# Two transformer blocks on one core: norms, a feed-forward entry and the last group in another order, six PSUM banks for the up-projection, and TensorE work in its pauses

## What is computed

```python
def rmsnorm(x, gain):
    var = jnp.mean(x * x, axis=-1, keepdims=True)
    return x * lax.rsqrt(var + 1e-6) * gain

# layer 1, its end
x = x + rmsnorm(merged @ w_out, norm_mix_post)
h = rmsnorm(x, norm_ffn_pre)
up = h @ w_up                       # 1024 -> 2 * 2816
conv = conv_b + sum(conv_w[i] * shifted(up, 2 - i) for i in range(3))
gate, val = jnp.split(conv, 2, axis=-1)
f = (gelu(gate) * val) @ w_down     # layers 2 and 3: silu in place of gelu
x = x + rmsnorm(f, norm_ffn_post)
# layer 2 begins with proj = rmsnorm(x, fox_norm) @ w_fox_in
# layer 3: v = (latent @ w_uv), 16 heads of 128
# the end
out = rmsnorm(x, final_norm)
```

## Time and profile before

| | us |
|---|---|
| median of 3 runs | 2248.14 (2243.22 to 2248.35) |
| the profiled execution | 2245.98 |
| its span, first to last instruction | 2244.2 |
| TensorE busy | 2174.7, 97% of the span |
| VectorE, ScalarE, GpSimd busy | 1176.3, 903.1, 934.9 |
| share of the chain that ended last | TensorE 89%, VectorE 6%, ScalarE 3%, DMA 1% |

### The profile page before, as it was taken

One profiled execution on the slowest core, in us unless ns is written; L12 is line 12 of the kernel. 1 busy time (PEld: TensorE's weight loads), 2 busy tenths in 40 slices (PEclk: granted clock), 3 DMA queues, 4 the chain that ended last, 5 costly groups with the idle time before them and its releaser, 6 DMA issues.

```text
span 2244.2 us, 26145 instructions
## 1 busy us (share of the span) xinstructions
PE 2174.7 (97%) x10426; PEld 1784.7 (80%) x10426; DVE 1176.3 (52%) x1713; ACT 903.1 (40%) x1381; POOL 934.9 (42%) x726
## 2 busy tenths in 40 slices
PE   8999999988999998999999999999999999999997
PEld 6877788866888877777788888887888888888886
DVE  5775333567666106676466662167666424666511
ACT  5214432353433224576444332254445334433322
POOL 5333435534444443322444444453222244454442
PEclk9999999999999998999999999999999999999998
DMA  5221223322333332211333233322111233333332
GB/s 176 69 71 58 79 71 99 103 75 75 100 98 92 98 102 66 75 57 39 95 102 94 94 101 95 96 94 67 50 54 51 62 95 96 101 94 96 97 94 80
DMA packets 57913, 191.48 MB, mean 85 GB/s; under 512 B 6448, under 2 KB 8640, under 8 KB 57792
## 3 DMA queue, kind: packets, MB, share of 16 engines
q1 hardware_dynamic: 57792, 189.81, 26.9%
HBM read 187.69 MB, written 2.10 MB: 85 GB/s over the span
## 4 chain that ended last, share of the span: by engine, by line
PE 89%; DVE 6%; ACT 3%; DMA 1%; issue 1%; ACTq 0%; POOL 0%; DVEq 0%; SPq 0%
PE ps L572 25%; PE ps L574 25%; PE ps L573 25%; PE ps L1039 2%; PE ps L625 1%; PE ps L937 1%; PE ps L626 1%; PE ps L627 1%; DMA RAW<-weights 1%; PE ps L928 1%; DVE TURNED L1552 1%; PE ps L992 1%; DVE CV L1555 1%; PE ps L678 1%; PE ps L961 1%
## 5 line engine op out<-in xcount | busy, mean ns | idle before, releaser
L564 POOL TENSOR_TENSOR WLO<-RAW,WHI 128x512 fp32r<-128x512 f32 (+1 forms) x722 | 934.6, 1320 | 1278.5 <-ACT WHI L1127 1278.0
L1127 ACT ACTIVATE WHI<-RAW 128x1024 fp32r<-128x1024 f32 (+2 forms) x374 | 373.1, 1001 | 666.9 <-DMA RAW<-weights 491.1
L572 PE MATMUL ps<-HH,WHI 128*128 128x512 f32 x1200 | 476.2, 397 | 26.2 <-POOL WLO L564 9.1
L574 PE MATMUL ps<-HH,WLO 128*128 128x512 f32 x1200 | 469.4, 391 | 0.0
L573 PE MATMUL ps<-HL,WHI 128*128 128x512 f32 x1200 | 469.3, 391 | 0.0
L572 PEld LDWEIGHTS ps<-HH,WHI 128*128 128x128 f32 x1200 | 226.8, 189 | 79.0 <-issue 12.5
L1555 DVE SCALAR_TENSOR_TENSOR CV<-U,PAR,CV 128x512 f32<-128x512 f32 x264 | 267.5, 1033 | 8.5 <-ACT CV L1342 3.9
L573 PEld LDWEIGHTS ps<-HL,WHI 128*128 128x128 f32 x1200 | 226.9, 189 | 48.8 <-issue 2.4
L574 PEld LDWEIGHTS ps<-HH,WLO 128*128 128x128 f32 x1200 | 226.5, 189 | 47.8
L1552 DVE TENSOR_TENSOR U<-ps,RSTD 128x512 f32<-128x512 f32 x132 | 90.5, 688 | 247.6 <-PE ps L574 224.2
L573 PE MATMUL ps<-ACTL,WHI 128*128 128x512 f32 (+1 forms) x550 | 209.3, 381 | 0.0
(11 more groups left out here) (314 smaller groups left out, 3305.5 us busy)
## 6 DMA issues: line engine op xcount, KB each, us to landing
RAW<-weights SPq DMA_DIRECT2D x300, 512.0 KB, 3.5
RAW<-weights SPq DMA_DIRECT2D x48, 384.0 KB, 3.0
RAW<-weights SPq DMA_DIRECT2D x26, 256.0 KB, 2.6
X<-xT SPq DMA_DIRECT2D x4, 512.0 KB, 6.5
outT<-X SPq DMA_DIRECT2D x8, 256.0 KB, 2.2
RESET<-resets SPq DMA_DIRECT2D x1, 512.0 KB, 10.8
CS<-rope SPq DMA_DIRECT2D x1, 512.0 KB, 3.7
M8F<-masks SPq DMA_DIRECT2D x1, 448.0 KB, 10.0
```

Of the source, the lines that this page charges most:

```text
L564: pool.tensor_tensor(WLO[:, slot, w], RAW[:, slot, w], WHI[:, slot, w].bitcast(F32), ALU.subtract).then_inc(w_lo, 1)
L572: pe.matmul(out, wh, hh, start=first, stop=False)
L574: return pe.matmul(out, wl, hh, start=False, stop=last)
L1127: act.activation(WHI[:, slot, 0:cols], RAW[:, slot, 0:cols], ACT.Copy).then_inc(w_hi, 1)
```

## The change

- **Banks**: gate.q and val.q of all three feed-forward networks get banks 2 (q mod 3) and 2 (q mod 3) + 1. The other groups keep their alternation of 0 and 1.
- **TensorE work in pauses**: four fp32 matmuls of a zeroed tile ahead of the first product, and 24 bf16 matmuls of a mask (`keep_clock`) behind `stats_in_two` in both block norms. Their results are not read.
- **Block norms**: VectorE clears SUMSQ ahead of the wait for RSTD and not behind the first two `scaled`; ScalarE loads the Ln table ahead of the last square (`early_table`); the cast of one chunk stands behind the second high tile and not ahead of the first.
- **Entry of feed-forward 0**: `stats` comes 12 matmuls earlier; ScalarE's casts of gate.2 to val.3 stand in other places of q = 0.
- **Latent attention**: the values of pair 0 are computed ahead of the first pair, with a weight chunk of their own (375 chunks, not 374).
- **The last group**: the sums for the first half stand in the second half, behind its block 6; VectorE scales six tiles of the first half ahead of adding the second.

```diff
+    tokens(["mv0.0", "mv0.1"], "mv0", 0, 2 * LORA_K)
     for p in range(MLA_H // 2):
...
@@ bank_table
             b = 2 + int(group[-1])
+        elif group[:4] in ("gate", "val0", "val1", "val2"):
+            b = int(group.split(".")[1]) % 3 * 2 + (group[0] == "v")
         else:
             b, turn = turn, 1 - turn
@@ tensor
+            def keep_clock(n):
+                for _ in range(n):
+                    pe.matmul(ps[:, 6, :], M16[:, 0:P], M16[:, 0:T], start=True, stop=True)
...
+            pe.wait_ge(zeroed, 1)
+            for _ in range(4):
+                pe.matmul(ps[:, 7, :], QT[:, 0:P], QT[:, 0:T], start=True, stop=True)
...
             stats_in_two("mixpost", 8)
+            keep_clock(24)
...
                     for at in range(4):
-                        for name in UP0_HEAD:
+                        for n, name in enumerate(UP0_HEAD):
+                            if at == 3 and n == 2:
+                                stats(site, 8)
                             part(name, at, *h, by_tile(site))
-                    stats(site, 8)
...
             stats_in_two("ffnpost", 8)
+            keep_clock(24)
...
             group("qn.1", *CQ_)
+            mla_values(0)
             for p in range(MLA_H // 2 - 1):
...
+                        if n and k == 6:
+                            pe.wait_ge(sumsq, SQ_AT["final"] + KD + 1)
+                            for m, part_ in enumerate(TOKEN_HALVES):
+                                pe.matmul(ps[:, HALF_SUM[m], part_], ones, SUMSQ[:, part_], start=True, stop=False)
+                            last_sum(0)
                 mm.then_inc(half_done, 1)
...
+            last_sum(1)
@@ scalar
+            def early_table(func):
+                warmed[0] += 1
+                act.activation(WARM[:, :], con("one"), func).then_inc(warm, 1)
+                act.wait_ge(warm, warmed[0])
...
                 else:
+                    early_table(ACT.Ln)
                     act.wait_ge(lin_done, DONE[f"{stage}.{j}"])
                     square(j, j % 2, ps[:, BANK[f"{stage}.{j}"], :], site)
...
-            casts(chunk_of("gate0.0"))
-            each_tile(lambda j, k: (act.wait_ge(x_done, j + 1), h_tile(j, k, "ffnpre0", "ffnpre0")))
+            for j in range(KD):
+                act.wait_ge(x_done, j + 1)
+                h_tile(j, j % 2, "ffnpre0", "ffnpre0")
+                if j == 1:
+                    casts(chunk_of("gate0.0"))
...
-                        casts(chunk_of(name) + 3 if f or q > 1 else chunk_of("gate0.2") + 3 + q)
+                        if f or q:
+                            casts(chunk_of(name) + 3 if f or q > 1 else chunk_of("gate0.2") + 3 + q)
+                        elif m == 0:
+                            casts(chunk_of("val0.2"))
...
+                    if f == 0 and q == 0:
+                        casts(chunk_of("gate0.2") + 3)
@@ vector
+            dve.memset(QT[:, 0:T], 0.0).then_inc(zeroed, 1)
...
             def post_norm(site, nxt, done):
+                clear_sum(nxt)
+                dve.sem_inc(sumsq, 1)
                 scale_known(site)
-                dve.sem_inc(sumsq, 1)
...
                 scaled(1)
-                clear_sum(nxt)
...
             drain_q(1)
+            drain_values(0, 0)
+            drain_values(0, 1)
             query_lo(1).then_inc(head_ready, 1)
...
+            last_add(0)
+            last_scaled(0, range(6))
+            last_add(1)
+            last_scaled(0, range(6, KD))
+            last_scaled(1, range(KD))
```

More of the change, by code:

```diff
@@ L161, in linear_plan @@
             whole(f"qn.{a}", QLORA_K)
-        values = [(f"mv{p}.{half}", f"mv{p}", 0, 2 * LORA_K, 0) for half in range(2)]
+        values = [(f"mv{p}.{half}", f"mv{p}", 0, 2 * LORA_K, 0) for half in range(2)] if p else []
         if p < MLA_H // 2 - 1:
@@ L1353, in _ @@
             root("ffnpost", D, RSTD)
-            casts(chunk_of("fv0.0"))
-            each_tile(lambda j, k: (act.wait_ge(x_done, j + (KD + 1)), h_tile(j, k, "fox", "fox")))
+            for j in range(KD):
+                act.wait_ge(x_done, j + (KD + 1))
+                h_tile(j, j % 2, "fox", "fox")
+                if j == 1:
+                    casts(chunk_of("fv0.0"))
             casts(chunk_of("foxf"))
@@ L1380, in _ @@
             act.activation(FZ[:, 1, :], FZ[:, 1, :], ACT.Ln, bias=con("one")).then_inc(f_act, 1)
-            act.activation(WARM[:, :], con("one"), ACT.Exp).then_inc(warm, 1)
-            act.wait_ge(warm, 2)
+            early_table(ACT.Exp)
             casts(chunk_of("fv1.3") + 3)
@@ L1519, in _ @@
             query_hi(1)
-            casts(chunk_of("qn.1") + 3)
+            casts(chunk_of("mv0.0") + 3)
             for p in range(MLA_H // 2 - 1):
```

28 lines of the change are left out of this document (16 added, 12 removed).

## The result

The changed kernel takes 2231.74 us (median of 4 runs, 2229.13 to 2233.17); the kernel before takes 2245.91 beside it (4 runs). The ratio is 0.9931 with a 95% interval of 0.9919 to 0.9943: faster by 14.2 us. That is inside the forecast range of 2219 to 2236, and 5.7 us above the forecast of 2226. The profiled execution is the fastest of the four, 2229.13 with a span of 2227.3; against the 2245.98 and 2244.2 of before that is 16.9 us in the pair of traces, where the prediction's terms add up to 20.5.

The account below looks back on a forecast made before the run. TensorE, busy 97% of the span, bounds the kernel; only its pauses and slow stretches, some 70 us of 2244, can be saved. Terms sum to -20.5 from 2245.98, giving 2225.5, rounded up to 2226; range 2219 to 2236.

Parts of the forecast that it names:

- start: Program start: fp32 matmuls ahead bring full clock, so seven slow first products run faster, -1.4 us.
- norm behind wout, first product: Block norm behind wout: VectorE's savings of 1.75 against Ln's +0.5 bring the first product 1.25 us earlier.
- the same norm, tiles behind it: Low tiles behind wout's norm: half clock saved, -1.9, against a wait for the fourth tile, +1.2; -0.7 us.
- feed-forward 0, wait and clock: Gate.4 no longer waits for gate.3's bank, -8.4 - 0.2, and the half clock behind goes, -2.1 us.
- late weights of val.4: Feed-forward 0: val.4's cast stands behind round 2 on ScalarE, so TensorE waits +0.6 us, between 0 and 3.
- three drains just begun: Starts of gate1.0, down0.0 and down1.0: each waits 0.95 us for a bank just left, +2.85 us in all.
- norm behind down0: Second block norm: Ln +1.3, VectorE -1.75, clock -2.45, wait for the fourth tile +1.2; -1.7 us in all.
- latent attention: Pair 0's values moved ahead: scores start 3.1 us later, 2.8 of products leave, full clock saves 3.0; -2.5 us.
- end: Last group: first-half sums and six scalings run beside the second half's products, -5.7 us, between -4.5 and -6.3.
- dear: Rival, both norms: 24 filling products at fp32 price overrun the first low tile, +28.6 us, 2254; chance 0.02.
- Cycling through six banks: Rival, gate and val groups: idles at bank changes bring half clock, 4.9 us a group, change ends slower; chance 0.02.
- the pauses still cost the clock: Rival, start, norms and latent stage: the clock still falls in remaining pauses, 4.9 us, 2230 to 2231; chance 0.17.

Follow-up runs that it names:

- c3: Changed kernel without the four products of zeros at the program's start: 2232.82 us, ratio 0.9939 to the kernel before.
- a1: Changed kernel without the early Ln table load in the two block norms: 2226.47 us, ratio 0.9911 to the kernel before.
- b3: Changed kernel without the early Ln load and with the moved cast behind the sixth high tile in both norms: 2226.96 us, ratio 0.9915.
- a2: Changed kernel with gate and val groups in two alternating banks again: 2234.41 us, ratio 0.9943 to the kernel before.
- b4: Changed kernel with the weights of val.4 cast one group earlier in feed-forward 0: 2232.83 us, ratio 0.9939 to the kernel before.
- a4: Changed kernel with gate and val banks swapped in the third feed-forward and the two-bank turn reset ahead of down0.0: 2228.24 us, ratio 0.9918.
- b1: Changed kernel with the latent values of pair 0 back in the first pair's turn: 2233.52 us, ratio 0.9943 to the kernel before.
- b2: Changed kernel with the end undone, both half sums behind the last product and eight scalings ahead of the second add: 2237.16 us, ratio 0.996.
- a3: Changed kernel without the 24 filling matmuls in either norm: 2232.06 us, ratio 0.9935 to the kernel before.
- c1_best: Changed kernel with no early Ln load, later norm casts, earlier val.4 cast, rearranged banks and reordered latent casts and drain: 2222.82 us, ratio 0.9895.
- c2: c1_best without the 24 filling products behind each norm's sums: 2224.41 us, ratio 0.9902 to the kernel before.
- c4: c1_best with 27 filling products instead of 24 and six more ahead of the second norm's second tile: 2222.11 us, ratio 0.989.

## Why the prediction was right, and where it was not

Term by term, the prediction against the shift of the products in the pair of traces, and against the experiment that isolates it:

| term | predicted | pair of traces | experiment |
|---|---|---|---|
| start | -1.4 | -1.4 | 2.5 at product 40 (c3) |
| norm behind wout, first product | -1.25 | -1.2 | early load +0.8 of it (a1) |
| the same norm, tiles behind it | -0.7 | -0.2 | late cast gives 1.0 back (b3) |
| feed-forward 0, wait and clock | -10.7 | -10.7 | 7.4 by the banks alone (a2) |
| late weights of val.4 | +0.6 | +1.9 | 0.6 to be had back (b4) |
| three drains just begun | +2.85 | +3.3 | 2.8 (a4) |
| norm behind down0 | -1.7 | +0.2 | early load +1.7 to +2.7 (a1) |
| latent attention | -2.5 | -3.0 | 1.0 to 2.1 (b1) |
| end | -5.7 | -5.6 | 5.6 (b2) |
| in no term (behind product 1063) | | -0.2 | |
| sum | -20.5 | -16.9 | |

**Right:** the mechanism and size of the two large terms. The wait for gate.4's bank went as reckoned and nothing but the weights of val.4 came in its place, and the end was met within 0.1. The text gives all of the first to the banks; a2 shows that 3.3 of the 10.7 came with the other edits, which have VectorE's rounds begin earlier. VectorE's -1.75 in the two norms was right as well: the first product comes 1.8 us earlier against Ln than before, in both. The three short waits for a drain at the named groups, a cost that the change does not show on its face, were priced at 0.95 and measured at 0.93. The filling products cost 0.22 us each at full clock (5.13 us for 23 records) and ended by the first low tile, so they were not dear. Cycling through six banks did nothing to the clock (1.00 in the long stretch). The Trainium skill (TensorE: Matmul & The Clock Gate, A second HAM failure mode: psum-queue depth-cycling) tells of a kernel that lost throughput with such cycling. In this kernel no stretch shows it.

**Wrong, the norm behind down0** (-1.7 predicted, +0.2 found, the largest miss). The step was "the load and the small activation push it by 1.5, Ln by +1.3". The push was counted on ScalarE alone, and its 1.5 was 1.7 to 1.8. What fell through is TensorE's side of it: the pause in front of the last square's sum grew to 1.98 us, the clock stood at half behind it, the sum itself took 2.07 us instead of 1.12, and Ln came at +2.6 instead of +1.3. With VectorE's -1.8 the first product was 0.8 us late where -0.45 was reckoned. The clock's gain behind it was sized rightly (-2.35 for -2.45), the wait for the fourth tile was not (+1.75 for +1.2). About 1.0 of the miss hangs on when the clock fell: a3, b1, b2 and c3 have the early load and a full clock at that sum, and their norm gains 0.8 us against before. In such profiles the early load still costs 1.7. The step also read the table load of the old order as a cost that the new one could move; it was hidden behind the last square's sum, so moving it ahead could only lose. The prediction saw that for the first norm, in so many words, and priced it at +0.5 (0.6 in the pair of traces, 0.8 by a1).

**Wrong, the tiles behind the first norm** (-0.7 predicted, -0.2 found). "The moved cast now lengthens VectorE's later tiles by the same 1.35 us": it lengthened two operations by 1.04 and 1.09, 2.1 in all, and the fourth tile cost 1.7 instead of 1.2. In before, one of the two pieces had met a shorter overlap (1.09 instead of 0.74); moved into VectorE's unbroken chain, both pieces met their full one. The clock's gain was the -1.9 reckoned in the pair of traces; but it and the waits are not separate terms, since at half clock TensorE waits less at each tile, and a3 found the whole stretch only 0.7 worse without the filling products.

**Undersized, the late weights:** round 0 took 11.7 us (486.97 to 498.68), not 10.7. That is most of the step from +0.6 to the wait of 1.7 (1.9 in the shift of the products). The addends given for 27.8 make 27.6, so the term as written out is +0.4.

**Latent attention:** the sum was fair, the path was not. The wait is for weights (2.08 us) at the first value product, with the drain only just behind it (c1_best shows that drain at 2.34 once the weights are early), and the clock still fell for 3.4 us, where the text took it as full. That -3.0 came out beside -2.5 is partly luck: the fall in the one profile of before lasted 6.8 us, that of b1 with the old order 3.4, and b1 puts the move at 1.0 to 2.1.

**The rival "the pauses still cost the clock"** at 2230 to 2231 came closest to the median. It had the right symptom but not this place: the clock fell ahead of the filling products and in the latent stage, and the waits for the fourth tile were not hidden. Two of its four supposed losses, the start and the first norm's clock, did not occur.

The rest of the distance between 2226 and 2231.74 lies in the first stage. The median execution of the changed kernel is 2.6 us longer than the profiled one, at granted clocks of 0.994 to 0.996 over the span in the other three, instead of 0.997; they have no trace, but the kernels with the same first stage show falls at 46 and 278 us, and first columns up to 4.5 longer. The kernel before has one profile, without them, and how often it has them is not known; its profiled execution is a typical one (2245.98 against medians of 2245.91 to 2246.99, of 4 to 9 runs).

Not settled: what decides whether the clock falls at a given pause. The pause of 1.86 to 2.04 us that the early load makes behind down0 stands in eight profiles; within 1 us behind it the clock fell in four (the changed kernel's, a2, a4, b4), early enough to lengthen the sum in two of them (2.07 and 1.65 us). Waits of 0.87 and 1.59 us behind 24 filling products led to half clock in a1 and b3, and to none in c1. The early falls also stay unexplained.

## What to carry to other kernels

A table load that already stands beside another engine's work is free; pulled ahead of that work it lengthens the path (by 0.8 and 1.7 us here), and the clock can fall at the pause that it makes. When operands of one engine are moved in time, follow what they set off: here a cast put in a better place on ScalarE sent two GpSimd pieces into VectorE's tightest chain, and more banks for one kind of group made three others start on a bank just left; both came back by choosing the place (a cast four tiles later, a different parity), for 1 and 2.8 us. Filling products save only what TensorE would not have spent waiting anyway: behind a norm whose tiles come every 2.5 us they brought between 0 and 2.2 us a norm, not the whole slow stretch.

## What the runs showed of the hardware

- Some 10 us at half clock behind a norm cost no more than 2.2 us (77.85 in c2 for 75.66 in c4) and once nothing (325.30 in a3 for 325.29 with a fall of 3.4 us), where TensorE is fed a tile every 2.5 us at either clock.
- Pauses of the same length, at the same place and behind the same work, leave the granted clock at 1.00 in one execution and at 0.50 in another; the pause behind down0 is one case (1.98 us and 0.50 in the changed kernel, 1.92 us and 1.00 in a3). The falls inside the kernel last 3.4, 6.8, 10.2 or 13.7 us in the traces here. Two profiles of one program part differ by 4.5 us in 290 where these falls are the difference seen, so single spans are a poor measure of a term of 1 or 2 us, and times between numbered products a better one.
- Two VectorE operations with both inputs in SBUF take 1.78 and 1.77 us instead of 0.74 and 0.68 while two GpSimd pieces run (2.99 us for the two, 2.50 elsewhere), wherever the pieces are moved: a cost of 2.1 us for each chunk that falls into a chain of such operations.
- A table load of 1.28 us is followed by the next instruction 0.01 us later in the changed kernel too (827.90 + 1.28, then 829.19): no drain behind it shows.
